# Attention over eight heads: four loop passes of two heads, or one chain of 32 steps with the mask added in a rounded format

## The chip, the cores and the metric

The kernel runs on one core of a Trainium2 chip. Its time is the device time of one execution in microseconds (us). The engines have short names: PE is the matrix engine (TensorE), DVE the vector engine, ACT the scalar engine, POOL is GpSimd and SP the engine that issues the loads. Each takes its instructions in order and waits for the others at semaphores.

## What is computed

The reference is two transformer-like blocks on 512 rows of 1024 values: matrix products with modulation, convolutions, feed-forward layers, and in the middle one attention over 8 heads of 64 values with a decay term and a causal mask. Only that attention is touched by the change.

```python
def forgetting_attention(q, k, v, f_logit, q_g, k_g):
    ...
    q = rms_norm(q, q_g)
    k = rms_norm(k, k_g)
    scale = 1.0 / math.sqrt(dh)
    c = jnp.cumsum(jax.nn.log_sigmoid(f_logit.astype(jnp.float32)), axis=1)
    ...
    def one_block(args):          # one block of 128 queries, all heads
        q_blk, cq_blk, blk = args
        q_pos = blk * Q_BLOCK + jnp.arange(Q_BLOCK)
        s = jnp.einsum("bhqd,bhkd->bhqk", q_blk, k_h).astype(jnp.float32) * scale
        s = s + cq_blk[..., :, None] - c_k[:, :, None, :]
        mask = k_pos[None, :] <= q_pos[:, None]
        s = jnp.where(mask[None, None], s, -jnp.inf)
        p = jax.nn.softmax(s, axis=-1)
        return jnp.einsum("bhqk,bhkd->bhqd", p.astype(v_h.dtype), v_h)
```

## The kernel before, in words

Everything lives in one program. Each engine has one hand-written list of instructions, and its order is the order in the code. The large products (`product`, lines 1270 to 1272) split each float32 operand into a high and a low half in the format float32r and add three products. Attention stands between the products of `even_w_in` and `even_w_out`. Its operands are in plain float32.

A step is one block of 128 queries of one head. Its query block sees 1 to 4 blocks of keys, so its score row is n = 128, 256, 384 or 512 wide. A step passes through the engines in this way:

- PE multiplies `QS` by `KS` into a PSUM bank (line 1442), and adds the causal mask by a second product, `IDENT` times `MASK` (line 1443). The scores carry the opposite sign, so the mask holds +1e30 and the row minimum is wanted.
- DVE takes the row minimum (line 1089). ACT computes the exponential from PSUM into `PR` with the row sum beside it (line 638).
- PE turns `PR` block by block (line 1451, 1 to 4 transposes). ACT copies the result into `PT` (line 645). PE multiplies `PT` by `V` (line 1459), one product for each key block. DVE takes the reciprocal of the row sum (line 1092) and scales the output into `OT` (line 1097).

The engines work on different steps at the same time. In one turn s of its loop PE issues the scores of step s, the transposes of step s-2 and the value product of step s-3; ACT does the exponential of s and the copy of s-2; DVE the minimum of s, the reciprocal of s-2 and the scaling of s-4. `QS` and `KS` have two slots, one for each head of a pair. `PR`, `PT` and the banks behind them have two slots each as well, and the scores have four banks.

A hardware loop (`Fori`) runs this four times, once for each pair of heads, with 8 steps in it. At its start DVE scales the operands of both heads (lines 1081 and 1083, four instructions), and ACT copies a decay row into `QS` and one into `KS` for each head (lines 630 and 631). PE begins a pass with `keep_busy(3, 2)`: three products of 512 columns whose result nobody reads (line 1289). In a pass the last steps drain before the next pass begins. Semaphore waits inside are against a value held in a register (`pair * 8 + s`).

POOL sums sliding windows over other data (`UP`, lines 411 and 417) while the first pair runs. `IDENT` is also the operand of all transposes of the kernel, and `MASK` is filled with another constant after attention and used again later.

Of the kernel before, what the change touches and what calls it, by code (L numbers as in the profile page):

```python
# [20 lines left out]
F32 = mybir.dt.float32  # L21
# [96 lines left out]
def program(nc, i, out):  # L118
    ctx = ExitStack()
    with ctx:  # L120
# [52 lines left out]
        IDENT = at("IDENT", 204.75, [P, P])  # L173
        ONES = at("ONES", 205.25, [P, P])
        BD = at("BD", 205.75, [P, P])
        MASK = at("MASK", 206.25, [P, P])
# [202 lines left out]
        def _(pool):  # L379
            for m, v in ((IDENT, 0.0), (ONES, 1.0), (BD, 0.0), (MASK, 0.0)):  # L380
                pool.memset(m[:, :], v).then_inc(s_const0, 1)
            pool.memset(sc_(S_EPS), EPS).then_inc(s_const, 1)
            pool.wait_ge(s_const0, 4)
            pool.affine_select(out=IDENT[:, :], in_=IDENT[:, :], compare_op=ALU.not_equal, fill=1.0, base=0,
                               pattern=[[-1, P]], channel_multiplier=1).then_inc(s_const, 1)

            pool.affine_select(out=MASK[:, :], in_=MASK[:, :], compare_op=ALU.is_ge, fill=MASKED, base=0,
# [34 lines left out]
            pool.memset(MASK[:, :], -1.0 / P).then_inc(g_k, 1)  # L422
# [39 lines left out]
        def _(act):  # L462
# [163 lines left out]
            with act.Fori(0, HEADS // 2) as pair:  # L626
                for h in range(2):
                    act.wait_ge(e_cr, 32)
                    act.wait_ge(a_qk, pair * 4 + (2 * h + 2))
                    act.activation(QS[64:65, h:h + 1, :], CR[64:65, ds(pair * 2 + h, 1), :], ACT.Copy).then_inc(a_row, 1)  # L630
                    act.activation(KS[96:97, h:h + 1, :], CR[96:97, ds(pair * 2 + h, 1), :], ACT.Copy).then_inc(a_row, 1)
                for s in range(10):
                    if s < 8:
                        n = (s % 4 + 1) * P
                        act.wait_ge(a_min, pair * 8 + (s + 1))
                        if s >= 2:
                            act.wait_ge(a_t, pair * 8 + (s - 1))
                        act.activation(PR[:, s % 2, 0:n], PS_[:, S_BANKS[s % 4], 0:n], ACT.Exp, scale=-1.0,
                                       bias=sc_(S_MN + s), accum_out=sc_(S_RS + s)).then_inc(a_e, 1)
                    if s >= 2:  # L640
                        k, n = s - 2, ((s - 2) % 4 + 1) * P
                        act.wait_ge(a_t, pair * 8 + (k + 1))
                        if k >= 2:
                            act.wait_ge(a_o, pair * 8 + (k - 1))
                        act.activation(PT[:, k % 2, 0:n], PS_[:, 4 + k % 2, 0:n], ACT.Copy).then_inc(a_tc, 1)
# [92 lines left out]
            for n in range(DC):  # L738
# [9 lines left out]
                for k in range(TAPS_PE[n]):  # L748
                    act.activation(DG[:, j, k, :], IDENT[:, :], ACT.Copy,
                                   scale=col("dw_w0", 8 * (TAPS - TAPS_PE[n] + k) + n)).then_inc(g_d, 1)  # L750
# [50 lines left out]
        def _(dve):  # L801
# [275 lines left out]
            with dve.Fori(0, HEADS // 2) as pair:  # L1077
                for h in range(2):
                    lo, hi = h * DH, h * DH + DH

                    stt(QS[0:DH, h:h + 1, :], QK[lo:hi, ds(pair, 1), :], small[lo:hi, S_Q8:S_Q8 + 1],
                        SQT[lo:hi, ds(pair, 1), :], ALU.mult, ALU.mult).then_inc(a_qk, 1)
                    stt(KS[0:DH, h:h + 1, :], QK[lo:hi, ds(pair + 4, 1), :], col("k_g")[lo:hi, :],
                        SQT[lo:hi, ds(pair + 4, 1), :], ALU.mult, ALU.mult).then_inc(a_qk, 1)
                for s in range(12):
                    if s < 8:
                        n = (s % 4 + 1) * P
                        dve.wait_ge(a_s, pair * 8 + (s + 1))
                        dve.tensor_reduce(sc_(S_MN + s), PS_[:, S_BANKS[s % 4], 0:n], AX.X, ALU.min).then_inc(a_min, 1)
                    if 2 <= s < 10:  # L1090
                        dve.wait_ge(a_e, pair * 8 + (s - 1))
                        dve.reciprocal(sc_(S_RR + s - 2), sc_(S_RS + s - 2)).then_inc(a_rr, 1)
                    if s >= 4:
                        k = s - 4
                        dve.wait_ge(a_o, pair * 8 + (k + 1))
                        dve.wait_ge(a_rr, pair * 8 + (k + 1))
                        dve.tensor_scalar(OT[:, k % 4, ds(pair * P + k // 4 * DH, DH)], PS_[:, k % 2, 0:DH],
                                          sc_(S_RR + k), None, ALU.mult).then_inc(a_oe, 1)
# [156 lines left out]
        def _(pe):  # L1255
# [30 lines left out]
            def keep_busy(n, bank=7):  # L1286

                for _ in range(n):
                    pe.matmul(PS_[:, bank, :], IDENT[:, :], VCOL[:, 0:T], start=True, stop=True)

# [31 lines left out]
            for t in range(VT):  # L1322
# [5 lines left out]
                pe.transpose(PS_[:, 6 + t % 2, 0:n], VROW[0:n, t, :], IDENT[0:n, 0:n]).then_inc(s_vt, 1)  # L1328
                if t == 0:
                    pe.wait_ge(s_xin, 16)  # L1330
                    for c in range(DC):
                        if c >= 4:
                            pe.wait_ge(s_xe, c - 3)
                        for b in range(TB):
                            tr = pe.transpose(PS_[:, c % 4, b * P:b * P + P], XROW[:, b, c * P:c * P + P], IDENT[:, :])
                        tr.then_inc(s_xt, 1)
# [95 lines left out]
            with pe.Fori(0, HEADS // 2) as pair:  # L1432
                keep_busy(3, 2)
                for s in range(11):
                    if s < 8:
                        h, qb, n = s // 4, s % 4, (s % 4 + 1) * P
                        pe.wait_ge(a_qk, pair * 4 + (2 * h + 2))
                        pe.wait_ge(a_row, pair * 4 + (2 * h + 2))
                        if s >= 4:
                            pe.wait_ge(a_e, pair * 8 + (s - 3))  # L1440
                        bank = PS_[:, S_BANKS[s % 4], :]
                        pe.matmul(bank[:, 0:n], QS[:, h, qb * P:qb * P + P], KS[:, h, 0:n], start=True, stop=True)  # L1442
                        pe.matmul(bank[:, n - P:n], IDENT[:, :], MASK[:, :], start=False, stop=True,
                                  skip_group_check=True).then_inc(a_s, 1)
                    if 2 <= s < 10:
                        k = s - 2
                        pe.wait_ge(a_e, pair * 8 + (k + 1))
                        if k >= 2:
                            pe.wait_ge(a_tc, pair * 8 + (k - 1))
                        for b in range(k % 4 + 1):  # L1450
                            tr = pe.transpose(PS_[:, 4 + k % 2, b * P:b * P + P], PR[:, k % 2, b * P:b * P + P], IDENT[:, :])
                        tr.then_inc(a_t, 1)
                    if s >= 3:
                        k = s - 3
                        pe.wait_ge(a_tc, pair * 8 + (k + 1))
                        if k >= 2:
                            pe.wait_ge(a_oe, pair * 8 + (k - 1))
# [180 lines left out]
```

## Time and profile before

| | us |
|---|---|
| median of 3 runs | 1844.48 |
| lowest | 1842.78 |
| highest | 2548.79 |
| the profiled execution, its own time | 1842.85 |
| its span, first to last instruction | 1841.1 |

The span is what the rows of the trace are measured in; the time of the execution is 1.75 us longer. The highest of the three runs stands apart from the other two, which lie 1.7 us from each other. PE is busy for 95% of the span. "Idle before" in a row is the time that the engine stood still just ahead of the instruction, and the name behind it is what it waited for.

### The profile page before, as it was taken

What the parts mean: (1) busy time and instruction counts of PE and PEld (TensorE: products, weight loads), DVE (VectorE), ACT (ScalarE), POOL (GpSimd) and SP (SyncE); (2) the same over time, 40 slices, a digit from 0 to 9 for tenths busy, and PEclk for the clock granted to TensorE, in tenths of its full rate; (3) what the DMA queues carried; (4) which work ended last, traced back from release to release, by engine and by line L of the source; (5) the groups of instructions that cost most, each with busy time, mean ns of one, the idle gap of its engine ahead of it and who ended that gap; (6) DMA issues with size and microseconds to landing.
All of it is one profiled execution on the core that took longest, in us unless ns stands there. A gap on an engine that the chain in (4) does not pass through costs nothing.

```text
span 1841.1 us, 21801 instructions
## 1 busy us (share of the span) xinstructions
PE 1754.4 (95%) x7714; PEld 1404.7 (76%) x7714; DVE 1081.0 (59%) x1647; ACT 692.5 (38%) x1000; POOL 132.3 (7%) x131
## 2 busy tenths in 40 slices
PE   4899999999999879989999999999998999999998
PEld 4788857888888658666888888877664788888887
DVE  5698846343434543545566474567998667366374
ACT  2222225231314232454443242344665454244242
POOL 0000000000000000300000000000896000000000
PEclk7799999999999989999999999999999999999999
DMA  7577412223333203200322223223221222323222
GB/s 237 161 228 229 138 46 91 92 92 94 107 96 108 69 23 115 70 1 3 106 97 92 91 91 114 91 69 92 69 69 46 69 92 91 109 81 107 91 80 80
DMA packets 182188, 176.14 MB, mean 96 GB/s; under 512 B 3160, under 2 KB 181596, under 8 KB 182124
## 3 DMA queue, kind: packets, MB, share of 16 engines
q1 hardware_dynamic: 182124, 175.29, 29.8%
q8 instruction: 39, 0.64, 0.2%
q14 instruction: 25, 0.20, 0.0%
HBM read 173.15 MB, written 2.10 MB: 95 GB/s over the span
## 4 chain that ended last, share of the span: by engine, by line
PE 89%; DVE 5%; issue 2%; ACT 2%; DMA 1%; DVEq 0%; SPq 0%; ACTq 0%
PE PSUM L1270 24%; PE PSUM L1272 24%; PE PSUM L1271 24%; PE PSUM L1544 2%; PE PSUM L1563 1%; PE PSUM L1565 1%; PE PSUM L1564 1%; PE PSUM L1315 1%; PE PSUM L1442 1%; PE PSUM L1459 1%; DMA XROW<-in_x 1%; DMA ARAW<-in_ada_w 1%; DVE SQ L821 1%; PE PSUM L1300 1%; PE PSUM L1356 0%
## 5 line engine op out<-in xcount | busy, mean ns | idle before, releaser
L472 ACT ACTIVATE WH<-RAW 128x1024 fp32r<-128x1024 f32 x280 | 287.1, 1052 | 766.9 <-PE PSUM L1272 749.4
L1270 PE MATMUL PSUM<-XH,WH 128*128 128x512 f32 x1232 | 483.1, 392 | 11.8 <-issue 10.8
L1271 PE MATMUL PSUM<-XL,WH 128*128 128x512 f32 x1232 | 480.3, 390 | 0.0
L1272 PE MATMUL PSUM<-XH,WL 128*128 128x512 f32 x1232 | 480.2, 390 | 0.0
L808 DVE TENSOR_TENSOR WL<-RAW,WH 128x1024 fp32r<-128x1024 f32 x280 | 342.3, 1246 | 10.0 <-ACT WH L472 9.4
L1270 PE MATMUL PSUM<-HH,WH 128*128 128x512 f32 x756 | 296.7, 393 | 8.1 <-DVE HL L1151 4.9
L1271 PE MATMUL PSUM<-HL,WH 128*128 128x512 f32 x756 | 295.5, 391 | 0.0
L1272 PE MATMUL PSUM<-HH,WL 128*128 128x512 f32 x756 | 295.2, 390 | 0.0
L1270 PEld LDWEIGHTS PSUM<-XH,WH 128*128 128x128 f32 x1232 | 231.9, 188 | 64.2 <-issue 15.6
L1271 PEld LDWEIGHTS PSUM<-XL,WH 128*128 128x128 f32 x1232 | 232.0, 188 | 49.0 <-issue 1.2
L1272 PEld LDWEIGHTS PSUM<-XH,WL 128*128 128x128 f32 x1232 | 231.8, 188 | 48.6
L1270 PEld LDWEIGHTS PSUM<-HH,WH 128*128 128x128 f32 x756 | 142.6, 189 | 41.1 <-DVE WL L808 5.7
L1272 PEld LDWEIGHTS PSUM<-HH,WL 128*128 128x128 f32 x756 | 142.6, 189 | 30.0
L1271 PEld LDWEIGHTS PSUM<-HL,WH 128*128 128x128 f32 x756 | 142.7, 189 | 29.5
L1127 DVE TENSOR_TENSOR ZP<-PSUM,R 128x512 f32<-128x512 f32 x88 | 56.7, 686 | 176.8 <-PE PSUM L1272 176.8
L891 DVE TENSOR_TENSOR X<-PSUM,X 128x512 f32 (+1 forms) x62 | 39.9, 685 | 158.5 <-PE PSUM L1272 152.4
L431 POOL TENSOR_TENSOR CP<-CP,PRD 128x512 f32<-128x512 f32 x68 | 93.0, 1367 | 458.8 <-ACT PRD L763 450.2
L1138 DVE SCALAR_TENSOR_TENSOR TA<-ZP,VCOL,TA 128x512 f32<-128x512 f32 x176 | 120.1, 743 | 0.0
L1203 DVE SCALAR_TENSOR_TENSOR PSUM<-UPAD,VCOL,PSUM 128x512 f32<-128x512 f32 x121 | 81.8, 747 | 0.4
L836 DVE SCALAR_TENSOR_TENSOR MACC<-ARAW,small,MACC 128x256 f32<-128x256 f32 x140 | 67.9, 485 | 5.0
L1004 DVE TENSOR_SCALAR TA<-PSUM 128x512 f32<-128x512 f32 x32 | 20.6, 685 | 84.9 <-PE PSUM L1272 84.9
L685 ACT ACTIVATE TA<-ZP,VCOL 128x512 f32<-128x512 f32 x88 | 66.7, 805 | 0.0
(237 smaller groups left out, 1671.5 us busy)
## 6 DMA issues: line engine op xcount, KB each, us to landing
RAW<-in_ffn_w_up SPq DMA_DIRECT2D x44, 1024.0 KB, 5.1
ARAW<-in_ada_w SPq DMA_DIRECT2D x24, 1024.0 KB, 5.3
RAW<-in_mlp_w_in SPq DMA_DIRECT2D x16, 1024.0 KB, 5.3
RAW<-in_mlp_w_out SPq DMA_DIRECT2D x16, 1024.0 KB, 4.9
RAW<-in_ffn_w_down SPq DMA_DIRECT2D x16, 1024.0 KB, 5.1
RAW<-in_sc_w_in SPq DMA_DIRECT2D x12, 1024.0 KB, 5.1
RAW<-in_even_w_in SPq DMA_DIRECT2D x8, 1024.0 KB, 5.4
RAW<-in_odd_w_pw SPq DMA_DIRECT2D x16, 512.0 KB, 4.7
```

The costliest lines, as they stand in the source:

```text
L431: pool.tensor_tensor(CP[:, n, :], CP[:, n, :], PRD[:, before % RING, :], ALU.add).then_inc(g_a, 1)
L472: act.activation(WH[:, j, a:b, :], RAW[:, j, a:b, :], ACT.Copy).then_inc(s_hi, 1)
L685: act.activation(TA[:, c, :], ZP[:, c, 2:T + 2], ACT.Identity, scale=col(f"fw{layer}2", it * 2 + (half + 2 * first + c)), bias=col(f"fb{la ...
L808: tt(WL[:, j, a:b, :], RAW[:, j, a:b, :], WH[:, j, a:b, :].bitcast(F32), ALU.subtract).then_inc(s_lo, 1)
L836: stt(dst, w, s, dst, ALU.mult, ALU.add).then_inc(s_as if k < 7 else s_ad, 1)
L891: ins = dve.tensor_copy(d, src) if first else tt(d, src, d, ALU.add)
L1127: tt(ZP[:, c, 2:T + 2], banks(j, c), R[:, :], ALU.mult).then_inc(f_z, 1)
L1138: stt(TA[:, c, :], ZP[:, c, tap:tap + T], col(f"fw{layer}{tap}", it * 2 + (half + 2 * first + c)), TA[:, c, :], ALU.mult, ALU.add).then_in ...
L1203: stt(acc, src, w, acc, ALU.mult, ALU.add).then_inc(g_v, 1)
L1270: pe.matmul(o, wh, mh[:, k, :], start=(k == 0), stop=False)
L1271: pe.matmul(o, wh, ml[:, k, :], start=False, stop=False)
L1272: mm = pe.matmul(o, wl, mh[:, k, :], start=False, stop=(k == kn - 1))
```

## The change

The loop over pairs is written out as one list of 32 steps on PE, ACT and DVE, over heads and blocks. The steps of different pairs overlap as those inside a pair did. The waits are against constants. The operands of heads 0 and 1 are made ahead of the chain. Those of head n (2 to 7) are made inside it: DVE scales them (`scaled_head`) after its share of step 4(n-1), and ACT copies the decay rows (`decay_rows`) after its share of step 4(n-1)+1, into the slot that head n-2 has left. `keep_busy(3, 2)` stands once ahead of the chain. `IDENT` and `MASK` are declared float32r, so that the mask product is one instruction in the rounded format; all other uses read the same bytes as float32 (`bitcast`).

```diff
-        IDENT = at("IDENT", 204.75, [P, P])
+        IDENT = at("IDENT", 204.75, [P, P], F32R)
-        MASK = at("MASK", 206.25, [P, P])
+        MASK = at("MASK", 206.25, [P, P], F32R)
...
-            with act.Fori(0, HEADS // 2) as pair:
-                for h in range(2):
-                    act.wait_ge(e_cr, 32)
-                    act.wait_ge(a_qk, pair * 4 + (2 * h + 2))
-                    act.activation(QS[64:65, h:h + 1, :], CR[64:65, ds(pair * 2 + h, 1), :], ACT.Copy).then_inc(a_row, 1)
...
+            def decay_rows(n):
+                act.wait_ge(e_cr, 32)
+                act.wait_ge(a_qk, 2 * n + 2)
+                act.activation(QS[64:65, n % 2, :], CR[64:65, n, :], ACT.Copy).then_inc(a_row, 1)
+                act.activation(KS[96:97, n % 2, :], CR[96:97, n, :], ACT.Copy).then_inc(a_row, 1)
+
+            decay_rows(0)
+            decay_rows(1)
+            for s in range(4 * HEADS + 2):
...
+                if s % 4 == 1 and 5 <= s < 4 * HEADS - 4:
+                    decay_rows(s // 4 + 1)
...
+            def scaled_head(n):
+                lo, hi, pair = n % 2 * DH, n % 2 * DH + DH, n // 2
+                if n >= 2:
+                    dve.wait_ge(a_s, 4 * n - 4)
+                stt(QS[0:DH, n % 2, :], QK[lo:hi, pair, :], small[lo:hi, S_Q8:S_Q8 + 1], SQT[lo:hi, pair, :],
+                    ALU.mult, ALU.mult).then_inc(a_qk, 1)
+                stt(KS[0:DH, n % 2, :], QK[lo:hi, pair + 4, :], col("k_g")[lo:hi, :], SQT[lo:hi, pair + 4, :],
+                    ALU.mult, ALU.mult).then_inc(a_qk, 1)
...
+                if s % 4 == 0 and 4 <= s < 4 * HEADS - 4:
+                    scaled_head(s // 4 + 1)
...
-            with pe.Fori(0, HEADS // 2) as pair:
-                keep_busy(3, 2)
-                for s in range(11):
+            keep_busy(3, 2)
+            for s in range(4 * HEADS + 3):
```

On PE, here is the end of a pass before, from the scores of its last step on. `ISA` and `REGISTER_ALU` rows are small steps that compute addresses and the values of waits.

```order
L1442 MATMUL PSUM<-KS,QS 128x512
L1443 MATMUL PSUM<-MASK,IDENT 128x128
L1447 REGISTER_ALU
L1451 MATMUL PSUM<-IDENT,PR 128x128 x2
L1459 ISA
L1459 MATMUL PSUM<-V,PT 128x64
L1447 REGISTER_ALU
L1451 MATMUL PSUM<-IDENT,PR 128x128 x3
L1459 MATMUL PSUM<-V,PT 128x64
L1459 ISA
L1459 MATMUL PSUM<-V,PT 128x64
```

The same place in the changed program, step 7 and what follows it:

```order
L1452 MATMUL PSUM<-KS,QS 128x512
L1453 MATMUL PSUM<-MASK,IDENT 128x128
L1461 MATMUL PSUM<-IDENT,PR 128x128 x2
L1469 MATMUL PSUM<-V,PT 128x64
L1452 MATMUL PSUM<-KS,QS 128x128
L1453 MATMUL PSUM<-MASK,IDENT 128x128
L1461 MATMUL PSUM<-IDENT,PR 128x128 x3
L1469 MATMUL PSUM<-V,PT 128x64 x2
L1452 MATMUL PSUM<-KS,QS 128x256
L1453 MATMUL PSUM<-MASK,IDENT 128x128
```

Between the transposes and value products of the last steps of a pair now stand the scores of the next two, and the register steps are gone.

On DVE, before, the last scalings of a pass are followed by the loop's end, and its start is this:

```order
L1077 ISA
L1081 SCALAR_TENSOR_TENSOR QS<-QK,small,SQT 64x512
L1083 ISA
L1083 SCALAR_TENSOR_TENSOR KS<-QK,VCOL,SQT 64x512
L1081 ISA
L1081 SCALAR_TENSOR_TENSOR QS<-QK,small,SQT 64x512
L1083 ISA
L1083 SCALAR_TENSOR_TENSOR KS<-QK,VCOL,SQT 64x512
L1088 ISA
L1089 TENSOR_REDUCE small<-PSUM 128x1
```

In the changed program the operands of a head are scaled inside the list, here those of head 3, behind the scaling of step 4 and ahead of the minimum of step 9:

```order
L1098 TENSOR_REDUCE small<-PSUM 128x1
L1101 RECIPROCAL small<-small 128x1
L1106 TENSOR_SCALAR OT<-PSUM,small 128x64
L1087 SCALAR_TENSOR_TENSOR QS<-QK,small,SQT 64x512
L1089 SCALAR_TENSOR_TENSOR KS<-QK,VCOL,SQT 64x512
L1098 TENSOR_REDUCE small<-PSUM 128x1
L1101 RECIPROCAL small<-small 128x1
L1106 TENSOR_SCALAR OT<-PSUM,small 128x64
```

Two scalings moved to a place between the output scaling of one step and the minimum of the next.

On ACT the changed program has this around the decay rows of head 3:

```order
L641 ACTIVATE PR,small<-PSUM,small 128x128
L648 ACTIVATE PT<-PSUM 128x384
L641 ACTIVATE PR,small<-PSUM,small 128x256
L648 ACTIVATE PT<-PSUM 128x512
L630 ACTIVATE QS<-CR 1x512
L631 ACTIVATE KS<-CR 1x512
L641 ACTIVATE PR,small<-PSUM,small 128x384
L648 ACTIVATE PT<-PSUM 128x128
L641 ACTIVATE PR,small<-PSUM,small 128x512
```

The two row copies stand behind the copy of step 7 (128x512) and ahead of the exponential of step 10 (128x384); before they stood at the start of each pass.

## Rows read from the trace of the kernel before

**Rows 1.** The page, part 1: busy time, share of the span, instructions.

```profile
PE 1754.4 (95%) x7714; PEld 1404.7 (76%) x7714; DVE 1081.0 (59%) x1647; ACT 692.5 (38%) x1000; POOL 132.3 (7%) x131
```

**Rows 2.** Windows (us; busy PE, PEld, DVE, ACT, POOL; clock; DMA), one for each pair.

```profile
773.00:793.00 20.00, 16.23 (x98) 12.04 (x97) 10.11 (x29) 9.89 (x28) 11.34 (x32) 1.00 0.01 2
793.00:812.00 19.00, 16.49 (x98) 12.28 (x98) 9.15 (x29) 10.02 (x29) 0.00 (x0) 1.00 0.00 0
812.00:832.00 20.00, 18.09 (x98) 13.35 (x99) 9.45 (x29) 10.30 (x29) 0.00 (x0) 0.91 0.00 0
832.00:848.00 16.00, 13.91 (x94) 11.33 (x93) 6.53 (x25) 8.88 (x26) 0.20 (x1) 1.00 0.00 0
```

**Rows 3.** Timeline of PE, second pair (start, length, instruction, idle before).

```profile
789.39 2.79 PE L1289 MATMUL PSUM<-VCOL,IDENT 128*128 128x512 f32 x6
793.20 0.46 PE L1442 MATMUL PSUM<-KS,QS 97*128 97x128 f32 x2 [1.01 <-DVE KS L1083]
...
798.96 0.65 PE L1442 MATMUL PSUM<-KS,QS 97*128 97x256 f32 x2
799.45 0.39 PE L1443 MATMUL PSUM<-MASK,IDENT 128*128 128x128 f32 x2
799.67 0.60 PE L1451 MATMUL PSUM<-IDENT,PR 128*128 128x128 f32 x4
...
804.12 0.50 PE L1451 MATMUL PSUM<-IDENT,PR 128*128 128x128 f32 x3
805.77 0.66 PE L1459 MATMUL PSUM<-V,PT 128*128 x4 [1.15 <-ACT PT L645]
806.26 0.61 PE L1451 MATMUL PSUM<-IDENT,PR 128*128 128x128 f32 x4
...
808.50 2.79 PE L1289 MATMUL PSUM<-VCOL,IDENT 128*128 128x512 f32 x6
812.31 0.46 PE L1442 MATMUL PSUM<-KS,QS 97*128 97x128 f32 x2 [1.01 <-DVE KS L1083]
```

**Rows 4.** Timeline of PE and DVE: first score product, last output scaling.

```profile
772.74 0.46 PE L1442 MATMUL PSUM<-KS,QS 97*128 97x128 f32 x2 [1.85 <-DVE QS L1081]
...
847.63 0.28 DVE L1097 TENSOR_SCALAR OT<-PSUM,small 128x64 f32 x1 [0.89 <-PE PSUM L1459]
```

**Rows 5.** Timeline of DVE, second pair.

```profile
799.87 0.42 DVE L1089 TENSOR_REDUCE small<-PSUM 128x1 f32<-128x256 f32 x1 [1.34 <-PE PSUM L1443]
...
803.94 0.69 DVE L1089 TENSOR_REDUCE small<-PSUM 128x1 f32<-128x512 f32 x1 [1.28 <-PE PSUM L1443]
...
808.81 0.28 DVE L1097 TENSOR_SCALAR OT<-PSUM,small 128x64 f32 x1 [0.89 <-PE PSUM L1459]
809.33 0.74 DVE L1081 SCALAR_TENSOR_TENSOR QS<-QK,small,SQT 64x512 f32 x1 [0.24 <-issue]
810.00 0.73 DVE L1083 SCALAR_TENSOR_TENSOR KS<-QK,VCOL,SQT 64x512 f32 x1
```

**Rows 6.** Timeline of ACT, second pair.

```profile
802.44 0.58 ACT L638 ACTIVATE PR<-PSUM,small 128x384 f32<-128x384 f32 x1 [1.02 <-DVE small L1089]
...
804.66 0.69 ACT L638 ACTIVATE PR<-PSUM,small 128x512 f32<-128x512 f32 x1 [1.38 <-DVE small L1089]
...
805.34 0.75 ACT L645 ACTIVATE PT<-PSUM 128x256 f32<-128x256 f32 x2
...
811.54 0.63 ACT L631 ACTIVATE KS<-CR 1x512 f32 x1
```

**Rows 7.** Timeline of DVE, before the first pair.

```profile
772.57 1.55 DVE L1083 SCALAR_TENSOR_TENSOR KS<-QK,VCOL,SQT 64x512 f32 x1
```

**Rows 8.** Windows of 4 us after 824, and timeline of PE there.

```profile
824.00:828.00 4.00, 3.06 (x22) 2.92 (x22) 0.97 (x5) 1.80 (x5) 0.00 (x0) 0.87 0.00 0
828.00:832.00 4.00, 4.00 (x8) 1.68 (x8) 3.11 (x5) 1.25 (x2) 0.00 (x0) 0.70 0.00 0
...
828.16 3.91 PE L1289 MATMUL PSUM<-VCOL,IDENT 128*128 128x512 f32 x6
```

More of the change, by code:

```diff
@@ L1076, in _ @@
             dve.wait_ge(e_r, 8)
[L1077 to L1098, printed above, removed]
@@ new lines, in _ @@
+            scaled_head(0)
+            scaled_head(1)
+            for s in range(4 * HEADS + 4):
+                if s < 4 * HEADS:
+                    n = (s % 4 + 1) * P
+                    dve.wait_ge(a_s, s + 1)
+                    dve.tensor_reduce(sc_(S_MN + s % 8), PS_[:, S_BANKS[s % 4], 0:n], AX.X, ALU.min).then_inc(a_min, 1)
+                if 2 <= s < 4 * HEADS + 2:
+                    dve.wait_ge(a_e, s - 1)
+                    dve.reciprocal(sc_(S_RR + (s - 2) % 8), sc_(S_RS + (s - 2) % 8)).then_inc(a_rr, 1)
+                if s >= 4:
+                    k = s - 4
+                    dve.wait_ge(a_o, k + 1)
+                    dve.wait_ge(a_rr, k + 1)
+                    dve.tensor_scalar(OT[:, k % 4, k // 4 * DH:k // 4 * DH + DH], PS_[:, k % 2, 0:DH],
+                                      sc_(S_RR + k % 8), None, ALU.mult).then_inc(a_oe, 1)
+                if s % 4 == 0 and 4 <= s < 4 * HEADS - 4:
+                    scaled_head(s // 4 + 1)
@@ L1288, in keep_busy @@
                 for _ in range(n):
[L1289 removed]
+                    pe.matmul(PS_[:, bank, :], IDENT[:, :].bitcast(F32), VCOL[:, 0:T], start=True, stop=True)
             def channel_sum(stat):
@@ L1431, in _ @@
             pe.wait_ge(s_ev, U_EVEN + 8)
-            with pe.Fori(0, HEADS // 2) as pair:
-                keep_busy(3, 2)
-                for s in range(11):
[L1435 to L1457, printed above, removed]
-                        for b in range(k % 4 + 1):
-                            mm = pe.matmul(PS_[:, k % 2, 0:DH], PT[:, k % 2, b * P:b * P + P],
-                                           V[:, b, ds(pair * P + k // 4 * DH, DH)], start=(b == 0), stop=(b == k % 4))
-                        mm.then_inc(a_o, 1)
@@ new lines, in _ @@
+            keep_busy(3, 2)
+            for s in range(4 * HEADS + 3):
+                if s < 4 * HEADS:
+                    h, qb, n = s // 4, s % 4, (s % 4 + 1) * P
+                    pe.wait_ge(a_qk, 2 * h + 2)
+                    pe.wait_ge(a_row, 2 * h + 2)
+                    if s >= 4:
+                        pe.wait_ge(a_e, s - 3)
+                    bank = PS_[:, S_BANKS[s % 4], :]
+                    pe.matmul(bank[:, 0:n], QS[:, h % 2, qb * P:qb * P + P], KS[:, h % 2, 0:n], start=True, stop=True)
+                    pe.matmul(bank[:, n - P:n], IDENT[:, :], MASK[:, :], start=False, stop=True,
+                              skip_group_check=True).then_inc(a_s, 1)
+                if 2 <= s < 4 * HEADS + 2:
+                    k = s - 2
+                    pe.wait_ge(a_e, k + 1)
+                    if k >= 2:
+                        pe.wait_ge(a_tc, k - 1)
+                    for b in range(k % 4 + 1):
+                        tr = pe.transpose(PS_[:, 4 + k % 2, b * P:b * P + P], PR[:, k % 2, b * P:b * P + P], IDENT[:, :].bitcast(F32))
+                    tr.then_inc(a_t, 1)
+                if s >= 3:
+                    k = s - 3
+                    pe.wait_ge(a_tc, k + 1)
+                    if k >= 2:
+                        pe.wait_ge(a_oe, k - 1)
+                    for b in range(k % 4 + 1):
+                        mm = pe.matmul(PS_[:, k % 2, 0:DH], PT[:, k % 2, b * P:b * P + P],
+                                       V[:, b, k // 4 * DH:k // 4 * DH + DH], start=(b == 0), stop=(b == k % 4))
+                    mm.then_inc(a_o, 1)
@@ L1546, in taps @@
                 if n >= 2:
-                    mm = pe.matmul(o, MASK[:, :], CV[:, 0, :], start=False, stop=True)
+                    mm = pe.matmul(o, MASK[:, :].bitcast(F32), CV[:, 0, :], start=False, stop=True)
                 mm.then_inc(g_m, 1)
```

46 lines of the change are left out of this document (22 added, 24 removed).

## The prediction

> **What bounds the kernel now.** I read the head of the page first: PE is busy for 95% of the span of 1841.1 us [rows 1]. So a change pays only where PE stands still, or where it does work that can be dropped. The change touches attention alone, so the second view is a window over each pair of heads [rows 2]. It shows PE busy for some 16 to 18 of 19 to 20 us, but DVE for 9 to 10 and ACT for 10: none of the three is full, and of PE's share a part is the three idle products of `keep_busy`. The third view, PE's timeline in the second pair, shows why [rows 3]. Scores begin at 793.20. From 798.96 on PE works closely until 804.12, where it turns the exponentials of step 6. The next value product starts at 805.77, after 1.15 us of idle time, because it waited for the copy `PT` on ACT. Then the last three steps drain, and at 808.50 `keep_busy` begins. The next pair cannot start its scores before its operands exist: DVE ends the last output scaling at 809.1, begins `QS` at 809.33 and `KS` at 810.00 [rows 5], and ACT's copies of the decay rows follow. The distance from one pair's first score product to the next is 19.1 us (793.20 to 812.31), and of it 15.9 us run up to the last output scaling (808.81 + 0.28) [rows 3, 5].
>
> So attention pays, for each pair, a filling of the pipeline, a drain, and about 3 us in which operands are made and PE only keeps itself busy. From the first score product at 772.74 to the end of the last scaling, 847.63 + 0.28, it takes 75.2 us [rows 4]. All that follows waits for that end, since the next products need the attention's output, so what is taken off there comes off the end of the kernel.
>
> **The chain of 32 steps, its three pieces.** I build the new stretch from the second pair, which ran at the full clock of 2.4 GHz (granted clock 1.00) and without POOL [rows 2].
>
> *Filling.* From the first scores to those of step 5: 798.96 - 793.20 = 5.8 us. It holds the masks of steps 0 to 4, five; one of them is under a wait. A mask is two instructions 0.22 us apart in sum (799.45 to 799.67), so 0.11 us each [rows 3]. As one instruction it saves 0.11 us. Piece: 5.8 - 4 x 0.11 = 5.4 us.
>
> *A head in the middle.* From the scores of step 5 at 798.96, PE reaches the point at which the scores of step 8 would stand at 804.12. Before that point nothing is different in a chain, so 5.16 us. Then come the scores of step 8 (128 columns), a mask and three transposes, and then the value product of step 5, which waits for a row of events that begins with the scores of step 7: minimum 803.94, exponential 804.66, copy 805.34, product 805.77 [rows 3, 5, 6]. That row of events takes 1.83 us and what PE has to do in that time, the new scores included, takes 0.9 us. The scores of step 8 are thus free, under that wait, but the wait stays. The product is four instructions, and behind it, at 806.26, step 9 begins, where now the next transposes stand [rows 3]. A head takes 806.26 - 798.96 = 7.3 us with the old masks. The masks of steps 5, 6 and 7 are on the path, that of step 8 is under the wait: 7.3 - 3 x 0.11 = 7.0 us. From step 5 to step 29 there are six heads: 41.8 us with 6.97 each.
>
> *Drain.* From step 5's scores to the end of a pair it is 809.09 - 798.96 = 10.1 us, less three masks: 9.8 us [rows 3, 5].
>
> Sum: 5.4 + 41.8 + 9.8 = 57.0 us. The first pair was slower than the second by 1.35 us: its scores began at 772.74 and its `keep_busy` at 789.39, 16.65 us, against 808.50 - 793.20 = 15.30 us [rows 3, 4]. At that time DVE's operand scalings took 1.55 us where later they took 0.74 [rows 5, 7], beside POOL's sliding sums. I add it: 58.4 us.
>
> Saved: 75.2 - 58.4 = **16.8 us**. Against the profiled execution: 1842.85 - 16.8 = **1826 us**. The median of the three runs is 1.6 us above that execution and the lowest run equals it, so I make no correction.
>
> **What hides the operands.** In the chain `scaled_head` costs DVE 0.67 + 0.74 = 1.4 us for a head (809.33 to 810.00, then 0.73) [rows 5]. It stands ahead of the minimum of step 5, 9, and so on; at that place DVE was idle for 1.34 us (799.87) [rows 5]. That is a cover with almost nothing left. What is queued behind it is that minimum, and behind it the exponential. A lateness of 0.1 to 0.2 us at each of six heads would be 1 us. For head 2 the scaling falls near 779, still beside POOL, and may take 1.55 twice: 1.6 us more at the most. `decay_rows` costs ACT 2 x 0.63 = 1.27 us, ahead of an exponential before which ACT was idle for 1.02 us (802.44) [rows 6]. The 0.25 us over are absorbed, I take it, because the value product of that step comes after the longest scores; if not, 1.5 us. So both together lie between 0 and 4 us, and I take 0: both rows say that the gaps hold nearly all.
>
> **The mask.** The trace has no product of 128 columns in the rounded format. Its price lies between nothing (0.22 us saved) and that of the two it replaces. Each instruction in this stretch follows the one before at 0.11 us or so, whatever it does (four transposes last 0.60, three 0.50 [rows 3]), so I take 0.11. With 3 masks on the path in each of some 7 heads, the ends are 2.3 us to either side. The Trainium skill ("FP8 and Floating Point Precision", TensorE Precision Notes) says that true float32 makes four passes through the array and the reduced format reads truncated operands in one; by that, four passes of 128 columns would become one, and the saving could be 0.16 us for each mask, 1 us more in all. No row here shows the spacing going below 0.11.
>
> **Register steps.** PE, DVE and ACT lose the small instructions that compute wait values and addresses. Most run ahead of a wait and cost nothing. I give them 0, and at the most 0.3 us for a head, 2 us of gain.
>
> The forecast's own range from these: 1826 - 4 to 1826 + 4, that is 1822 to 1830.
>
> **Rivals.**
>
> *The wait for `PT` goes too (faster).* If PE never waited in the chain, 0.9 us for each of seven heads would go: 1826 - 6.6 = 1819.5. For it: register steps lie in that row of events. Against it: minimum, exponential and copy alone take 0.69 + 0.69 + 0.4 us, and the order on the engines is unchanged. Chance 0.08, 1817 to 1822.
>
> *The clock drops at the heads' boundaries.* In the third pair the granted clock fell: 0.87 and 0.70 in two windows, that is partly at 1.2 GHz, after a drain with its wait; the same `keep_busy` took 3.91 us there and 2.79 us after the first and second pairs [rows 3, 8]. So a stretch at the lower clock costs 1.1 us. The chain has no `keep_busy` between pairs, and a wait of 0.9 us at every head. For it speaks also that windows of a pair are uneven already. Against: the drains, where PE has only value products, are gone, and the three filled stretches are replaced by dense work. The Trainium skill ("TensorE: Matmul & The Clock Gate", A second HAM failure mode) has the rule that short idle times between groups of products, if frequent, make the clock oscillate; by it the chain would lose rather than win. The trace agrees in part, since one of four pairs was hit. With 3 to 7 boundaries hit: 3 to 8 us, 1829 to 1834. Chance 0.15.
>
> *The operands are not hidden.* The change would then not do what it says: 1.4 us on DVE and 1.27 us on ACT stand in the path of each of six heads, 16 us, and the time is 1842, no change. Against it speak the idle times of 1.34 and 1.02 us. Half of it would be 1834. Chance 0.06, 1831 to 1843.
>
> *The clock stays down through the chain (slower).* One place: the chain itself, without the filler products between pairs. PE's own work for a head is about 7.0 - 0.9 = 6.1 us; at half the clock 12.2, eight heads 98 us, with the ends 101 us against 75: 1842.85 + 26 = 1869. It decides against the change from about 17 us of PE work at the lower clock, a third of the chain. Against it: no window of attention before was below 0.70, the clock came back in the next one [rows 8]. Chance 0.03.
>
> **How the numbers follow.** Forecast 0.68 (1822 to 1830), clock at boundaries 0.15, wait gone 0.08, not hidden 0.06, clock down 0.03. The range that leaves out no more than 2 in 10: 1820 to 1834, which takes in the unknown costs and most of the clock case. A change of 2% (37 us), about what a measurement of this kernel can tell from none, is beyond all cases but the worst: even with PE never idle and no filling, attention would still need some 49 us of the 75. Faster by over 2%: 0.01; within 2%: 0.97; slower: 0.02.
>
> **What the changed profile would show.** The first score product to the last output scaling: 58 us, right within 2. Between the scores of steps 9 and 13: 7.0 us. One mask instruction for each step, the next instruction 0.11 us behind its start. At each head one wait of PE for `PT` of 0.8 to 1.0 us, and none for `QS` or `KS` after the start. DVE idle before the second minimum of a head falls from 1.34 to under 0.3 us. What would make it wrong: PE waiting for minimum or exponential at the second or third step of a head (cover too thin), or a granted clock under 0.95 in the windows of the chain.

## The result, and the profile after

The changed kernel takes 1835.46 us in the median of 6 runs (1834.15 to 1837.01), against 1843.77 us for the kernel before on the same chip. The ratio is 0.9944, 95% interval 0.9928 to 0.9961. That is faster by 0.6%, about half of what was forecast, and within the 2% of no change. The prediction said 1826 us and a range of 1820 to 1834; the median lies 1.5 us above the top of that range. (One of the six runs of before, at 2548.79 us, stands far apart; the ratio leaves it out.)

The profiled execution took 1837.01 us, the longest of the six. Its first score product starts at 774.63, 1.9 us later than in the trace of before (772.74). The change has no part in this, since DVE's write of `UP`, which stands ahead of the attention, is already later by as much (765.61 against 763.67). The head of its page follows. PE's share is what it was [rows 1]:

```profile
span 1835.2 us, 21490 instructions
...
PE 1751.2 (95%) x7664; PEld 1405.1 (77%) x7664; DVE 1079.5 (59%) x1647; ACT 692.0 (38%) x1000; POOL 133.2 (7%) x131
```

From the first score product (774.63) to the end of the last output scaling the attention now takes 67.6 us, where it took 75.2 [rows 4] and 58.4 were forecast:

```profile
841.93 0.28 DVE L1106 TENSOR_SCALAR OT<-PSUM,small 128x64 f32<-128x64 f32 x1 [0.89 <-PE PSUM L1469]
```

The windows over the chain, with the columns of [rows 2], say why it is not 58:

```profile
773.00:777.00 4.00, 1.82 (x9) 1.32 (x9) 3.97 (x6) 2.08 (x4) 3.80 (x3) 1.00 0.40 137
777.00:781.00 4.00, 3.04 (x9) 2.01 (x10) 0.93 (x4) 2.18 (x8) 3.73 (x4) 0.59 0.00 0
781.00:789.00 8.00, 8.00 (x33) 6.99 (x34) 3.38 (x12) 4.74 (x13) 6.02 (x25) 0.50 0.00 0
...
797.00:801.00 4.00, 4.00 (x16) 3.39 (x17) 0.81 (x3) 2.70 (x8) 0.00 (x0) 0.50 0.01 2
801.00:805.00 4.00, 4.00 (x14) 2.74 (x14) 1.66 (x7) 1.05 (x3) 0.00 (x0) 0.50 0.00 0
805.00:813.00 8.00, 7.32 (x52) 6.16 (x53) 5.47 (x17) 5.77 (x17) 0.00 (x0) 1.00 0.00 0
```

The granted clock falls just before 778 (the mean of the window from 777 to 781 is 0.59) and stays at 0.50, that is at 1.2 GHz, until 805. Then it is full for the rest. Before, the first pair ran at 1.00 throughout [rows 2]; there was one stretch of a few us at the lower clock, in the third pair [rows 8].

PE's timeline shows both parts of the chain:

```profile
774.63 0.46 PE L1452 MATMUL PSUM<-KS,QS 97*128 97x128 f32 x2 [1.93 <-DVE QS L1087]
...
777.96 0.47 PE L1461 MATMUL PSUM<-IDENT,PR 128*128 128x128 f32 x1 [1.51 <-ACT PR L641]
778.23 1.92 PE L1452 MATMUL PSUM<-KS,QS 97*128 97x512 f32 x2
...
792.10 0.74 PE L1452 MATMUL PSUM<-KS,QS 97*128 97x128 f32 x2
...
803.40 0.74 PE L1452 MATMUL PSUM<-KS,QS 97*128 97x128 f32 x2
...
818.52 0.66 PE L1469 MATMUL PSUM<-V,PT 128*128 128x64 f32 x4 [0.69 <-ACT PT L648]
819.02 0.65 PE L1452 MATMUL PSUM<-KS,QS 97*128 97x256 f32 x2
...
819.57 0.60 PE L1461 MATMUL PSUM<-IDENT,PR 128*128 128x128 f32 x4
...
825.35 0.66 PE L1469 MATMUL PSUM<-V,PT 128*128 128x64 f32 x4 [0.68 <-ACT PT L648]
825.84 0.65 PE L1452 MATMUL PSUM<-KS,QS 97*128 97x256 f32 x2
```

At full clock, a head from step 17 to step 21 (819.02 to 825.84) takes 6.82 us. At the lower clock, step 8 to step 12 (792.10 to 803.40) take 11.30 us. PE's wait for the copy `PT` is there at each head of the fast part, 0.68 us, and at the start the wait for the first exponential is 1.51 us, at the end of which the products run at the slow rate. In the kernel before this wait was 1.12 us, because the scores and masks ahead of it kept PE busy for longer:

```profile
776.07 0.33 PE L1451 MATMUL PSUM<-IDENT,PR 128*128 128x128 f32 x1 [1.12 <-ACT PR L638]
```

From the first scores to this transpose both kernels take 3.33 us; PE is busy for 2.21 of them before and for 1.82 now.

The operands made in the chain show on DVE, at the place of the first row of [rows 5]:

```profile
811.29 0.75 DVE L1087 SCALAR_TENSOR_TENSOR QS<-QK,small,SQT 64x512 f32<-64x512 f32 x1
811.96 0.75 DVE L1089 SCALAR_TENSOR_TENSOR KS<-QK,VCOL,SQT 64x512 f32<-64x512 f32 x1
812.95 0.42 DVE L1098 TENSOR_REDUCE small<-PSUM 128x1 f32<-128x256 f32 x1 [0.23 <-PE PSUM L1453]
```

They are made in the gap; the minimum behind them still waits for PE, 0.23 us, where the gap was 1.34.

### The profile page after: what moved, and what is told of

It is laid out like the page before. It is cut to its first block, busy times and chain, and to the rows that moved or that the text cites. A ratio compares the mean times of both kernels' runs of the same rounds, so it can differ in the third digit from the quotient of the medians.

```text
span 1835.2 us, 21490 instructions
## 1 busy us (share of the span) xinstructions
PE 1751.2 (95%) x7664; PEld 1405.1 (77%) x7664; DVE 1079.5 (59%) x1647; ACT 692.0 (38%) x1000; POOL 133.2 (7%) x131
## 4 chain that ended last, share of the span: by engine, by line
PE 90%; DVE 5%; ACT 2%; issue 2%; DMA 1%; DVEq 0%; SPq 0%; ACTq 0%
PE PSUM L1281 24%; PE PSUM L1283 24%; PE PSUM L1282 24%; PE PSUM L1554 2%; PE PSUM L1573 1%; PE PSUM L1575 1%; PE PSUM L1574 1%; PE PSUM L1452 1%; PE PSUM L1469 1%; PE PSUM L1326 1%; DMA XROW<-in_x 1%; PE PSUM L1461 1%; DMA ARAW<-in_ada_w 1%; PE PSUM L1367 1%; DVE SQ L826 1%
## 5 line engine op out<-in xcount | busy, mean ns | idle before, releaser
L1281 PEld LDWEIGHTS PSUM<-XH,WH 128*128 128x128 f32 x1232 | 231.8, 188 | 65.2 <-issue 15.9
```

The source lines that it names most:

```text
L1281: pe.matmul(o, wh, mh[:, k, :], start=(k == 0), stop=False)
```

## The experiments

Eleven kernels were run, in three groups; each group shares its runs of the kernel before (median 1848.3, 1844.4 and 1844.5 us). "Chain" is the time from the first score product to the end of the last output scaling in the profiled execution, and "heads" the distances between the 128-column scores of successive heads. "Low" is the stretch at 1.2 GHz in that execution, in attention and its drain. "Clock" is the granted clock as a mean over the whole execution, the lowest and the highest of all runs of the kernel: it is the only sign of a low stretch in the runs that were not profiled.

| kernel | median us | ratio to before (95%) | chain us | heads us | low | clock |
|---|---|---|---|---|---|---|
| before | 1843.8 | | 75.2 | 20.5, 19.1, 19.7 a pair | 3 us, third pair | 0.973 to 0.978 |
| changed | 1835.5 | 0.9944 (0.9928 to 0.9961) | 67.6 | 6.2, 11.3, 11.3, 6.8 ... | 27 us from 778 | 0.970 to 0.972 |
| mask_only | 1850.4 | 1.0020 (1.0004 to 1.0036) | 79.8 | 27.8, then 18.0 and 18.3 a pair | 24 us from 776, 7 us from 851 | 0.968 to 0.971 |
| chain_only | 1829.4 | 0.9907 (0.9877 to 0.9936) | 60.9 | 5.0, 7.3 ... | none | 0.978 to 0.979 |
| kb_start | 1833.7 | 0.9927 (0.9902 to 0.9952) | 67.6 | 6.2, 11.3, 11.3, 6.7 ... | 27 us from 776 | 0.969 to 0.970 (three), 0.976 (three) |
| kb_head | 1834.2 | 0.9937 (0.9913 to 0.9962) | 64.4 | 6.2, 11.3, 8.1, 6.8 ... | 17 us from 778 | 0.971 to 0.974 |
| mask_late | 1829.5 | 0.9912 (0.9880 to 0.9945) | 58.3 | 5.0, 7.2, 6.8 ... | 7 us from 830, after the last scores | 0.976 to 0.977 |
| mask_x4 | 1834.1 | 0.9946 (0.9929 to 0.9963) | 65.2 | 5.2, 7.9 ... | none | 0.974 to 0.978 |
| kb_fill | 1826.0 | 0.9900 (0.9866 to 0.9934) | 57.9 | 4.9, 7.3, 6.8 ... | none | 0.978, one 0.976 |
| loop_kb_once | 1849.5 | 1.0021 (1.0008 to 1.0034) | 81.0 | 21.1, 21.6, 20.8 a pair | 10 us from 788, twice 3 | 0.973 to 0.974 |
| same_ops | 1825.4 | 0.9887 (0.9861 to 0.9913) | 57.5 | 4.9, 6.7, 6.8 ... | none | 0.978 |
| pool_late | 1824.7 | 0.9884 (0.9858 to 0.9909) | 57.3 | 4.1, 7.5, 6.8 ... | none | 0.977 to 0.978 |
| mask_fill | 1843.6 | 0.9988 (0.9974 to 1.0001) | 74.1 | 19.8, 19.0, 19.5 a pair | 3 us, third pair | 0.976 to 0.979 |

The kernel before varies too: its 48 runs beside the experiments lie between 1842.6 and 1851.6 us, the shortest at a mean clock of 0.976 to 0.978 and 11 of them at 0.973 and about 1851 us. So in about one execution in four it takes some 8 us more, together with a lower clock; none of these was profiled, so where that happens is open. All rows of before in this document come from a short one.

### The two halves of the change: mask_only and chain_only

The theory after the first result: the pauses at the start of the chain let the clock fall, and the chain, without fillers, keeps it down. The rival: the shorter mask is what tips it.

**mask_only** is the kernel before with the declarations, bitcasts and the one-instruction mask.

```diff
-        IDENT = at("IDENT", 204.75, [P, P])
+        IDENT = at("IDENT", 204.75, [P, P], F32R)
-        MASK = at("MASK", 206.25, [P, P])
+        MASK = at("MASK", 206.25, [P, P], F32R)
```

> The kernel before (four loop passes) with the mask product in the rounded format and nothing else. Theory: some 7 of the 8 masks of a pair are on PE's path, 0.11 us each, so 0.7 us for a pair and 3 us in all: 1841 us against 1843.8, and the granted clock in attention as before (one short stretch below full at the most). Rival: the missing second instruction thins PE's work so much that the clock falls during the filling of a pair; then 1845 us or more with a clock under 0.9 in the windows of the first pair.

The theory's 1841 us did not come, the rival's number did: it is slower than the kernel before, by 0.2%, and all ten runs have a lower mean clock (0.968 to 0.971) than any of before. Its windows:

```profile
775.00:779.00 4.00, 2.82 (x8) 1.79 (x9) 0.92 (x3) 2.38 (x8) 3.69 (x5) 0.60 0.00 0
779.00:792.00 13.00, 12.52 (x49) 10.08 (x48) 3.66 (x17) 5.21 (x16) 5.85 (x27) 0.50 0.01 2
792.00:799.00 7.00, 7.00 (x26) 5.45 (x26) 2.66 (x6) 0.89 (x2) 0.00 (x0) 0.50 0.00 0
```

So the loop, with its fillers between pairs, falls too, at the same place of its first pair. The next two pairs, at full clock, take 18.0 and 18.3 us in place of 19.1: there the mask pays 0.8 to 1.1 us a pair. The clock falls once more in the last drain, at 851 for 7 us; the chain is 4.6 us longer than before (79.8 us, its last output scaling ends at 852.65), and what stands behind it 2.4 us.

**chain_only** is the changed kernel with the plain mask.

```diff
-                    pe.matmul(bank[:, n - P:n], IDENT[:, :], MASK[:, :], start=False, stop=True,
+                    pe.matmul(bank[:, n - P:n], IDENT[:, :].bitcast(F32), MASK[:, :].bitcast(F32), start=False, stop=True,
```

> The changed kernel with the mask product back in plain float32 (two instructions), the chain of 32 steps kept. Theory: the pauses at the chain's start (waits for the operands and for the first exponential) let the clock fall, and the chain without filler products keeps it down; the mask has no part in it. Then a stretch of 20 to 30 us at 1.2 GHz again and about 1838 us, 2 to 3 us over the changed kernel. Rival: the shorter mask is what tips the clock; then the clock stays up and the time is about 1829 us, under the changed kernel.

The rival's number came, 1829. The clock stays at 1.00 in every window of the chain; the first three:

```profile
773.00:777.00 4.00, 2.34 (x13) 1.85 (x14) 3.20 (x6) 2.28 (x6) 3.82 (x3) 1.00 0.12 42
777.00:781.00 4.00, 3.35 (x22) 2.61 (x23) 2.56 (x7) 2.89 (x11) 3.68 (x5) 1.00 0.00 0
781.00:789.00 8.00, 7.35 (x54) 6.29 (x53) 5.23 (x17) 4.92 (x14) 6.02 (x25) 1.00 0.01 2
```

My theory fell: the chain's own pauses do not lower the clock as long as the mask is two instructions. But the mask changes a pause too: with the plain one the wait for the first exponential is 1.13 us here, not 1.51. The chain alone is faster than the whole change.

### Where work has to stand: kb_start, kb_head, kb_fill

**kb_start** has two more fillers ahead of the first scores.

```diff
-            keep_busy(3, 2)
+            keep_busy(5, 2)
```

> The changed kernel with five filler products instead of three ahead of the chain; the two more fit into the 1.9 us in which PE waits for the first operands. Theory (the pause at the start is the trigger): the clock stays at full and the time is about 1826 us. Rival (the wait of 1.5 us for the first exponential, or the thin scores themselves, is the trigger): no change, about 1835 us, clock down from about 777 us on.

```profile
771.43 1.88 PE L1300 MATMUL PSUM<-VCOL,IDENT 128*128 128x512 f32 x4
773.52 0.46 PE L1452 MATMUL PSUM<-KS,QS 97*128 97x128 f32 x2 [0.21 <-DVE QS L1087]
...
776.86 0.48 PE L1461 MATMUL PSUM<-IDENT,PR 128*128 128x128 f32 x1 [1.51 <-ACT PR L641]
777.12 1.92 PE L1452 MATMUL PSUM<-KS,QS 97*128 97x512 f32 x2
```

The fillers take up the wait ahead of the scores, now 0.21 us, and the products behind the wait of 1.51 us are slow all the same (the 512-column scores last 1.92 us). In the profiled execution nothing was gained. The runs fall into two groups, though: three at 1836.0 to 1838.5 us with a mean clock of 0.969 to 0.970, like the changed kernel's, and three at 1830.8 to 1831.4 with 0.976. By that mean, most of the low stretch was absent in half of the runs. None of those was profiled, so what the two fillers did in them is open, and work ahead of the scores cannot be called without effect.

**kb_head** has one filler in PE's wait for `PT` at each head.

```diff
+                if s % 4 == 0 and 8 <= s < 4 * HEADS:
+                    keep_busy(1, S_BANKS[1])
```

> The changed kernel with one filler product of 512 columns in the wait for the copy at each of the steps 8, 12, ... 28 (six fillers; PE waits there 0.7 us at full clock). Theory: the clock falls at the start as in the changed kernel, but comes back with one of the first fillers, since what keeps it down is the chain's thin work; 1829 to 1832 us. Rival: fillers only add work (0.2 to 0.9 us each), the clock stays down as long as before: 1836 to 1840 us.

```profile
792.27 0.74 PE L1452 MATMUL PSUM<-KS,QS 97*128 97x128 f32 x2
...
793.57 1.76 PE L1300 MATMUL PSUM<-VCOL,IDENT 128*128 128x512 f32 x2
795.17 0.56 PE L1471 MATMUL PSUM<-V,PT 128*128 128x64 f32 x4
795.56 0.65 PE L1452 MATMUL PSUM<-KS,QS 97*128 97x256 f32 x2
```

In the profiled execution the low stretch ends with the first filler it meets: the filler starts at 793.57 and behind it four value products last 0.56 us and the 256-column scores 0.65, the full rate. The stretch was 17 us instead of 27, and the chain 3.2 us shorter. The median of 1834.2 us is 2 us above the 1829 to 1832 that were expected and about that of the changed kernel, since the low clock was still there for the first heads; two of the five runs have its mean clock too (0.971). The heads with a filler at full clock take 6.82 us, so it is free there.

**kb_fill** has one filler in the wait for the first exponential, once.

```diff
+                if s == 2:
+                    keep_busy(1, S_BANKS[3])
```

> The changed kernel with one filler product of 512 columns in PE's wait of 1.5 us for the first exponential (behind the mask of step 2). Theory (the idle time in the filling is the trigger, and work there cures it, where two fillers ahead of the scores did not): no low stretch, 1826 us. Rival (the clock falls for a reason that lies in the format or in the chain behind): a low stretch of 20 us or more again, 1834 to 1837 us.

```profile
774.29 0.52 PE L1453 MATMUL PSUM<-MASK,IDENT 128*128 128x128 f32 x1
774.65 1.07 PE L1300 MATMUL PSUM<-VCOL,IDENT 128*128 128x512 f32 x2
776.32 0.33 PE L1463 MATMUL PSUM<-IDENT,PR 128*128 128x128 f32 x1 [0.60 <-ACT PR L641]
776.49 1.03 PE L1452 MATMUL PSUM<-KS,QS 97*128 97x512 f32 x2
```

1826.0 us, the forecast. The filler leaves 0.60 us of the wait, and the scores behind it run at the full rate (1.03 us). The chain takes 57.9 us. So what the changed kernel's chain lost against the forecast is this low stretch, and a filler worth 0.9 us in one place takes it away. (One of the four runs took 1830.64 us at a mean clock of 0.976.)

### Format or amount: mask_x4 and mask_late

**mask_x4** issues the rounded mask four times.

```diff
+                    for _ in range(3):
+                        pe.matmul(bank[:, n - P:n], IDENT[:, :], MASK[:, :], start=False, stop=True,
+                                  skip_group_check=True)
```

> The changed kernel with the rounded mask product issued four times (the mask value becomes 4e30 in place of 1e30), so that as many columns pass as in one plain float32 product. Theory (the amount of work in the filling decides): the clock stays up; a step costs 0.1 to 0.3 us more than with one, and the time is 1830 to 1834 us with no low stretch. Rival (the format itself decides): the clock falls from about 777 us on as in the changed kernel, and the time is 1838 us or more.

```profile
775.06 0.74 PE L1454 MATMUL PSUM<-MASK,IDENT 128*128 128x128 f32 x3
775.64 0.27 PE L1456 MATMUL PSUM<-MASK,IDENT 128*128 128x128 f32 x1
776.43 0.33 PE L1464 MATMUL PSUM<-IDENT,PR 128*128 128x128 f32 x1 [0.51 <-ACT PR L641]
```

No low stretch, with the format unchanged: the rounded format as such does not lower the clock. The products added here also shorten the wait for the first exponential, from 1.51 to 0.51 us, so it stays open whether more work or a shorter wait keeps the clock up. The three extra products are the 1.0 us that a head is longer (7.87 against 6.82), so the time is no better than the changed kernel's. Four of the ten runs, at 1836.5 to 1841.7 us, have a mean clock of 0.974 to 0.977 where the others have 0.978: in them the clock was low somewhere, and no trace shows where.

**mask_late** has the plain mask in the first head alone.

```diff
+                    mi, mk = IDENT[:, :], MASK[:, :]
+                    if s < 4:
+                        mi, mk = mi.bitcast(F32), mk.bitcast(F32)
```

> The changed kernel with the plain float32 mask for the first head (steps 0 to 3) and the rounded one from step 4 on. Theory: what lets the clock fall is only the filling of the chain, where PE has three score products, three masks and a wait; a running chain with rounded masks holds the clock. Then no low stretch, heads of 6.8 us, and 1826 us, 3 us under the kernel with the plain mask throughout. Rival: the rounded format in the chain lowers the clock wherever it is used; then a low stretch in some later head and 1833 to 1838 us.

```profile
777.00:781.00 4.00, 3.21 (x27) 2.89 (x26) 3.55 (x8) 2.04 (x8) 3.67 (x5) 1.00 0.00 0
...
813.00:832.00 19.00, 16.04 (x109) 13.58 (x109) 9.35 (x33) 10.19 (x31) 0.21 (x1) 0.94 0.01 2
```

The low stretch at the start is gone and all later heads run rounded at 6.82 us; seven heads with the short mask and its waits never lowered the clock. The chain takes 58.3 us. In this execution the clock fell for 7 us after the last scores, in the drain (the 0.94), and what stands behind the chain took 2.8 us more than in kb_fill. That is most of what the expected 1826 us was missed by: the runs lie at 1828.2 to 1828.5 and at 1830.4 to 1830.9, and the longer ones were not profiled.

### What the fillers between pairs did: loop_kb_once

```diff
+            keep_busy(3, 2)
             with pe.Fori(0, HEADS // 2) as pair:
-                keep_busy(3, 2)
```

> The kernel before with its three filler products once ahead of the loop and none at the start of the later pairs. PE is then idle for the 3 to 4 us between pairs. Theory (fillers between pairs are what brings the clock back in a loop with drains): the clock falls at a pair's start and stays low for 10 us or more in some pairs; 1855 to 1875 us. Rival (the fillers do nothing there): 1843 us as before, with the same one short stretch.

```profile
777.00:792.00 15.00, 11.07 (x77) 9.46 (x76) 6.41 (x22) 5.75 (x18) 7.32 (x28) 0.88 0.01 2
792.00:799.00 7.00, 5.46 (x15) 4.00 (x16) 2.86 (x6) 4.17 (x11) 0.00 (x0) 0.52 0.00 0
...
812.00:832.00 20.00, 15.20 (x91) 12.32 (x92) 8.98 (x27) 10.06 (x28) 0.00 (x0) 0.91 0.00 0
```

Slower by 0.2%, with low stretches around the starts of pairs 2, 3 and 4. The longest begins in the drain of pair 1, at 788, and lasts 10 us (0.88 and 0.52 in the first two windows); the other two last 3 us each. Without the fillers between pairs the clock falls at each of the three boundaries, where in the trace of before it fell at one, so they hold it there for the most part, but the price of their absence is small: 5 us, not the 11 to 31 that were expected. A pair needs 20.8 to 21.6 us.

### The hidden costs: same_ops, pool_late, mask_fill

**same_ops** is kb_fill without the operands of heads 2 to 7; those heads use the operands of heads 0 and 1 again, so the output of six heads is another one.

```diff
-                if s % 4 == 0 and 4 <= s < 4 * HEADS - 4:
-                    scaled_head(s // 4 + 1)
...
-                if s % 4 == 1 and 5 <= s < 4 * HEADS - 4:
-                    decay_rows(s // 4 + 1)
```

> The kernel kb_fill (the changed kernel with one filler in the wait for the first exponential) without the operands made inside the chain: heads 2 to 7 use the operands of heads 0 and 1 again, so twelve scalings on DVE and twelve row copies on ACT are left out. Theory: they were hidden; the heads stay at 6.8 us and the time at 1825 to 1826 us. Rival: they cost a part of each head, 0.3 us or more; then 1824 us or less, and heads of 6.5 us.

From the third head on the heads take 6.82 us with and without: 2.7 us of work for each is fully hidden. The second is shorter by 0.6 us (6.72 against 7.28), where DVE's scalings fall beside POOL's sums.

**pool_late** is kb_fill with POOL's sums held back.

```diff
             pool.wait_ge(s_mm, U_EVEN + 8)
+            pool.wait_ge(a_qk, 4)
             step = 0
```

> The kernel kb_fill with POOL's sliding sums held back until DVE has scaled the operands of heads 0 and 1. Theory: DVE's four scalings at the start take 0.74 us in place of 1.5, the scores begin 1.5 us earlier; the sums then lie beside the scalings of heads 2 and 3, whose cover is thin (0.2 to 0.4 us), and each of those may come 1.6 us late. Together 1824.5 to 1828 us. Rival: the scalings of heads 2 and 3 are not slowed enough to matter: 1824 us.

```profile
770.03 0.74 DVE L1088 SCALAR_TENSOR_TENSOR QS<-QK,small,SQT 64x512 f32<-64x512 f32 x1 [0.48 <-ACT SQT L625]
770.69 0.73 DVE L1090 SCALAR_TENSOR_TENSOR KS<-QK,VCOL,SQT 64x512 f32<-64x512 f32 x1
...
778.05 1.14 DVE L1088 SCALAR_TENSOR_TENSOR QS<-QK,small,SQT 64x512 f32<-64x512 f32 x1
779.12 1.52 DVE L1090 SCALAR_TENSOR_TENSOR KS<-QK,VCOL,SQT 64x512 f32<-64x512 f32 x1
```

The first scalings take 0.74 us, not 1.55 [rows 7]; those of head 2, now beside the sums, 1.14 and 1.52. It is the fastest of all: 1824.7 us, 1.4 us under kb_fill. Between these two the intervals overlap, but the start of the trace shows the gain: the scores begin 7.1 us after the start of DVE's last work on `UP` (765.80 to 772.94), 9.0 us in the changed kernel (765.61 to 774.63) and in kb_fill (763.97 to 772.99).

**mask_fill** is mask_only with the filler of kb_fill in each pair.

```diff
+                    if s == 2:
+                        keep_busy(1, S_BANKS[3])
```

> The kernel mask_only (four loop passes, rounded mask) with one filler product of 512 columns in PE's wait for the first exponential of each pair. Theory: the rounded mask's loss came only from the clock; with the filling covered the clock stays up and the mask pays 0.16 us for each of 6 to 7 masks of a pair, 4 us in all: 1839 to 1841 us. Rival: the loop loses for another reason (the drain): a low stretch again and 1846 us or more.

```profile
793.47 0.52 PE L1443 MATMUL PSUM<-MASK,IDENT 128*128 128x128 f32 x1
793.83 1.07 PE L1289 MATMUL PSUM<-VCOL,IDENT 128*128 128x512 f32 x2
794.74 0.27 PE L1453 MATMUL PSUM<-IDENT,PR 128*128 128x128 f32 x1
```

The low stretch at the start is gone again, so what helps in the chain helps in the loop. But 1843.6 us is 3 over what was expected, no measurable change from before. From the second pair on the filling has no wait at this place (here the transposes follow the filler at once), and the filler costs what it takes, 0.9 us a pair, about as much as the mask saves.

## Why the prediction was right and wrong

**The chain.** Its three pieces, 5.4 + 41.8 + 9.8 us and 1.35 for the first pair, made 58.4 us at the full clock. kb_fill, which differs from the changed kernel by one filler, has 57.9 us, and chain_only, with the old masks, 60.9, where the same sum without any saving of the mask gives 61.1 (58.4 + 25 masks x 0.11). The heads take 7.30 us with the plain mask, as laid out from the second pair. That kb_fill came so near is in part luck: with 0.16 us for each mask, as measured, the sum would be 57.1, and a dearer second head made up most of the rest (both below). Otherwise this part was right, and so was its reason: the wait for `PT` stays, with the new scores under it.

**The clock: the step that failed.** The prediction built the chain "from the second pair, which ran at the full clock" and gave the case of a lower clock 0.15, at 1.1 us for each head's boundary, with the reason that `keep_busy` is missing there. The step that failed is the piece *Filling*, which was taken at full clock, 5.4 us, with no term for what the shorter masks do to it. The runs showed something else in each of three points. The place was the filling of the chain and not a boundary: seven boundaries in mask_late and kb_fill never lowered it inside the chain. The cause was the other half of the change, the mask: mask_only falls at that place with all its fillers between pairs, chain_only does not. And the price was not 1.1 us: the low stretch, once begun, lasted 27 us, over the end of the filling and two heads of 11.3 us instead of 6.8, and cost 67.6 - 57.9 = 9.7 us, of the 16.8 that were forecast. The prediction weighed the mask for its duration alone, 0.11 us each, and never as work that PE would miss in a stretch where it already waits (1.82 us busy of 3.33 us up to the first transpose, where it was 2.21 before). That products put into that stretch keep the clock up is shown from three sides: by the plain masks (chain_only and mask_late), by more masks of the same format (mask_x4) and by a filler (kb_fill). But each of them also shortens the wait for the first exponential, to 1.13, 0.51 and 0.60 us from 1.51, and no run separates the work from the wait. Work ahead of the stretch with the same wait (kb_start) did not help in the profiled execution, and in half of the runs it seems to have. Why the low stretch lasted 27 us is shown in part: a filler of 512 columns ended it early (kb_head), and without one it ended at 805, among the value products of step 9, 2 us behind the 512-column scores of step 11; the same products one head earlier had not ended it. What brings the clock back stays open.

The Trainium skill's rule on short idle times between groups of products ("TensorE: Matmul & The Clock Gate", A second HAM failure mode), which the prediction named, fits the place, since the clock fell in a wait between thin products, but not the frequency: seven later waits of 0.7 us, one for each head, did not bring it down.

**The mask.** Taken at 0.11 us, it measured 0.16: a head is 6.82 us and not 6.97, (7.30 - 6.82) / 3. The trace of the changed kernel has the same: 819.02 to 819.57 for the scores, mask and turn to the transposes of step 17, 0.55 us, where before it was 0.71 (798.96 to 799.67) [rows 3]. The Trainium skill ("FP8 and Floating Point Precision", TensorE Precision Notes) was nearer: from its four passes for true float32, taken against one, the prediction had worked out 0.16 as an estimate.

**The operands.** Taken at 0 between 0 and 4 us; same_ops shows 0 for heads 3 to 7 and 0.6 us for head 2. The 1.6 us named as the most beside POOL was a third of that. The signs given for it came: DVE's idle time fell from 1.34 to 0.23 us.

**The first pair.** 1.35 us, from POOL's sums beside the scalings, was right in sum: from its first scores to those of step 5 chain_only takes 7.11 us (773.54 to 780.65), where the second pair took 5.76. With POOL's sums held back (pool_late) the scores begin 1.9 us sooner, a gain that the 75.2 us do not hold, and the chain is 0.6 us shorter.

**The rivals.** That the wait for `PT` goes did not happen, it is 0.68 us in each head. Operands that are not hidden and a chain wholly at the low clock did not happen. The range missed the median by 1.5 us, because it took in only part of the clock's case, and because that case was priced by the one short stretch that the trace of before held.

## What to carry to other kernels

When an edit makes PE's work shorter in a stretch where PE already waits (the filling of a pipeline, above all), ask what the granted clock will do there, and test each half of the edit by itself: here one half of a change was worth 14 us and the other took 6 of them back, while it would have given 3. A single dummy product inside the wait repaired it; two ahead of the scores did so in half of the runs at most, and one in each loop pass cost what the mask had saved. A price for a low clock taken from one short stretch says little of a longer one: the same 1.2 GHz cost 1.1 us in the trace of before and 9.7 here. Look at the mean clock of every run as well, since one profile shows one execution.

## What was not expected of the hardware

The low clock held for 27 us while PE was counted as busy 4.00 of 4.00 us in the windows (797 to 801 and 801 to 805 above). Being busy in the profile's sense did not bring the clock back. One filler of 512 columns did, within 1.6 us, in the trace of kb_head. A plain float32 mask of two instructions in place of one, 0.16 us more at three places, was enough to keep the clock up through all heads (chain_only and mask_late), with a wait of 1.13 us at that place in place of 1.51.
